# Expert stage of a decoder layer: split distance, whole f32 down weights, place of the row sums

## The chip, the cores and the metric

The program runs on one core of one Trainium2 chip. The metric is the device time of one execution in microseconds (us); less is better. Engines: PE (matmul; PEld loads its stationary side), DVE (vector), ACT (scalar), POOL (GpSimd), SP (issues most DMAs).

## The reference

A layer of [RMSNorm, four token mixers, gated merge, residual] and [RMSNorm, hierarchical mixture of experts, residual], then a last RMSNorm, on 512 tokens of width 1024, all in float32. The change touches the experts alone:

```python
gates = ...                      # (tokens, 16): top-1 group, top-2 experts in it
for e in range(N_EXPERTS):       # 16 experts, hidden 512
    h = jax.nn.silu(xt @ w_g[e]) * (xt @ w_u[e])
    out = out + gates[:, e:e + 1] * (h @ w_d[e]).astype(f32)
```

Each token goes to two experts only, so the kernel gathers the tokens of an expert and leaves the others out.

## The kernel before

The stages follow each other: mixers, merge, output projection, routing (to about 656 us), experts, closing part. Five engine programs are written out by hand; they meet through semaphores, and each works strictly in its written order.

**Split numbers.** The weights come in float32. A product is made of f16 halves: ACT writes the high half of a weight chunk (line 853, times 64), DVE the rest (line 1737, chunk minus high half), and `products` (lines 980 to 982) makes three f16 matmuls, high by high, high by low, low by high. The tokens x and the hidden values h are split the same way.

**Chunks.** The 16 experts' weights are 96 chunks of 128 x 2048 float32 (1 MB), listed in `STEPS`: for expert e two "g" (gate), two "u" (up), then two "d" (down) of expert e-1. Numbers: expert e's first g chunk is c = 6e-2 (for e above 0), its u chunks follow, then 6e+2 and 6e+3 are d of e-1. Before expert 14's u chunks the d chunks of 13 are taken first, so 84 and 85 are d of 13; 92, 93 are d of 14 and 94, 95 d of 15. A g or u chunk takes 16 x 3 matmuls of 96 columns (CAP = 96 places for tokens), a d chunk 4 x 3 of 512.

**Buffers and SP.** There are 12 stage slots (`NS`) for float32 chunks and six pairs of f16 halves (`NW`). `stage_load` (line 450) issues a chunk's DMA; before it SP waits until the slot's last chunk is split (`splits_ahead`), and loads are issued in order of c. From chunk 20 on the slot is that of c-12.

**ACT and DVE.** Both walk over the steps c. At step c they do the small work of that step, then `split(c + LOOK)`, with LOOK = 5. ACT's small work: after the second g chunk it waits for that chunk's products and makes the tanh (918); at the second u chunk it waits for the transposes of the next expert's x and writes its high halves (908); one step later the high half of h (928); after the second d chunk it waits for its products and copies y out (935; 939 for experts 14 and 15, whose rows stay on the chip). DVE's: x low halves (1844), h (1894, 1895), h low half (1849), y low halves (1859), the sums of rows (1854).

**PE.** At step c it waits for the split of c (and for x or h where a step begins with them), does the products and signals `chunk_used`. After the second u chunk it transposes the next expert's tokens (1322).

**Tokens.** POOL gathers an expert's tokens with an indirect DMA (580) and scatters its y rows of experts 0 to 13 to memory (588). At the end SP reads them back (494) in four groups of 128 tokens, and `add_rows(t)` adds two of them per token with their weights, at the last four steps c = 92 to 95, after that step's other work on DVE. Experts 14 and 15 come back by one-hot matmuls (`put_back`, 1367), which `add_last` (1916) adds; then the norm (897, 892, 1826, 1829) and the store (510).

Of the kernel before, what the change touches and what calls it, by code (L numbers as in the profile page):

```python
# [50 lines left out]
LOOK = 5  # L51
# [89 lines left out]

def steps_to(kind, e):

    return STEPS.index((kind, e, 1)) + 1
# [49 lines left out]
def build(nc, d, out):  # L196

    ctx = ExitStack()
    with ctx:
# [92 lines left out]
        def splits_ahead(c):  # L292

            return max((i + 1 for i in range(c) if SLOT[i] == SLOT[c]), default=0)
# [13 lines left out]
        hgT = [[view(19456 + 512 * i + 256 * j, KH * CAP // 2).bitcast(F16) for j in range(2)] for i in range(2)]  # L308
# [111 lines left out]
        def _(sp_):  # L420
# [47 lines left out]
            for c in range(READY, READY + FIRST):  # L468
                sp_.wait_ge(S("split_done"), splits_ahead(c))
# [10 lines left out]
            with sp_.If(fit):  # L480
                for c in range(READY + FIRST, len(STEPS)):
                    if splits_ahead(c):
                        sp_.wait_ge(S("split_done"), splits_ahead(c))
                    elif c == READY + FIRST:
                        sp_.wait_ge(S("x2_stored"), 16 * NT)
                    else:
                        sp_.wait_ge(S("token_full"), 2)
# [4 lines left out]
                for t in range(NT):  # L492
                    sp_.wait_ge(S("split_done"), len(STEPS) - NS + t + 1)
# [102 lines left out]
        def _(act):  # L596
# [252 lines left out]
            def split(c):  # L849
                act.wait_ge(S(f"stage_landed{SLOT[c]}"), landed(c))  # L850
                if c >= NW:
                    act.wait_ge(S("chunk_used"), c - NW + 1)
                act.activation(w_hi[c % NW], stage[c], ACT.Copy, scale=WSCALE).then_inc(S("hi_done"), 1)  # L853
# [48 lines left out]
            with act.If(fit):  # L902
# [10 lines left out]
                for c, (kind, e, hf) in enumerate(STEPS):  # L913
# [9 lines left out]
                    if STEPS[c - 1][0] == "u" and STEPS[c - 1][2]:  # L923
                        eh = STEPS[c - 1][1]
                        act.wait_ge(S("h_ready"), eh + 1)
                        if eh >= 2:
                            act.wait_ge(S("chunk_used"), steps_to("d", eh - 2))
                        act.activation(hgT[eh % 2][0], hid, ACT.Copy).then_inc(S("hhi_done"), 1)
                    if kind == "d" and hf:
# [3 lines left out]
                        for j in range(2):  # L933
                            if e < ROUTED:
                                act.activation(yout[e % 2][0:CAP, 512 * j:512 * (j + 1)], ps[4 + j][0:CAP, :], ACT.Copy,  # L935
                                               scale=1.0 / (WSCALE * HSCALE)).then_inc(S("y_out"), 1)
# [4 lines left out]
                    if FIRST <= c + LOOK < len(STEPS):  # L941
                        split(c + LOOK)
# [22 lines left out]
        def _(pe):  # L965
# [339 lines left out]
            with pe.If(fit):  # L1305
# [23 lines left out]
                for c, (kind, e, hf) in enumerate(STEPS):  # L1329
                    if kind == "d" and not hf:  # L1330
                        pe.wait_ge(S("hlo_done"), e + 1)
# [8 lines left out]
                    pe.wait_ge(S("split_done"), c + 1)  # L1340
                    if kind == "d":
                        v = [w[c % NW].rearrange("p (k n) -> p k n", k=2) for w in (w_hi, w_lo)]
                        hi, lo = (h.rearrange("p (k c) -> p k c", c=CAP) for h in hgT[e % 2])
# [627 lines left out]
```

## Time and profile before

| | us |
|---|---|
| median of 3 runs | 964.55 (960.51 to 964.68) |
| profiled execution, its own time | 964.39 |
| span of its trace | 962.6 |
| PE busy | 876.3 (91%) |
| DVE busy | 658.8 (68%) |
| ACT busy | 481.0 (50%) |
| mean granted clock of PE | 0.957 of 2.4 GHz |

Times in rows are microseconds from the span's start unless marked ns. A share of busy time is an average over stages with different limits. In a timeline "[0.98 <-DMA ...]" is idle time before the instruction and what ended it. DMA share is the mean over 16 DMA engines.

### The profile page before, as it was taken

What the parts mean: (1) busy time and instruction counts of PE and PEld (TensorE: products, weight loads), DVE (VectorE), ACT (ScalarE), POOL (GpSimd) and SP (SyncE); (2) the same over time, 40 slices, a digit from 0 to 9 for tenths busy, and PEclk for the clock granted to TensorE, in tenths of its full rate; (3) what the DMA queues carried; (4) which work ended last, traced back from release to release, by engine and by line L of the source; (5) the groups of instructions that cost most, each with busy time, mean ns of one, the idle gap of its engine ahead of it and who ended that gap; (6) DMA issues with size and microseconds to landing.
All of it is one profiled execution on the core that took longest, in us unless ns stands there. A gap on an engine that the chain in (4) does not pass through costs nothing.

```text
span 962.6 us, 19161 instructions
## 1 busy us (share of the span) xinstructions
PE 876.3 (91%) x8176; PEld 585.2 (61%) x8176; DVE 658.8 (68%) x877; ACT 481.0 (50%) x681; POOL 81.8 (8%) x89
## 2 busy tenths in 40 slices
PE   6999999999999998999999979948899999888683
PEld 4444794856756655444444439947687777776561
DVE  5668769632887766643453344466799999998878
ACT  5434473323554445233223223554597878787842
POOL 8000000003000000000000000000121232111100
PEclk9999999999999999999999999967899999999987
DMA  8711414526731012953432416374899999999852
GB/s 213 168 35 45 125 30 110 155 66 176 188 91 34 25 37 61 372 137 98 121 102 83 122 28 220 127 284 140 305 359 383 399 397 397 381 392 378 331 203 90
DMA packets 122607, 178.20 MB, mean 185 GB/s; under 512 B 13357, under 2 KB 98661, under 8 KB 114326
## 3 DMA queue, kind: packets, MB, share of 16 engines
q1 hardware_dynamic: 116272, 162.76, 49.6%
q0 software_dynamic: 5968, 13.61, 5.2%
q8 instruction: 66, 1.08, 0.5%
q10 hardware_dynamic: 278, 0.56, 0.2%
q14 instruction: 23, 0.19, 0.1%
HBM read 170.67 MB, written 14.39 MB: 192 GB/s over the span
## 4 chain that ended last, share of the span: by engine, by line
PE 64%; DVE 19%; DMA 7%; ACT 6%; issue 3%; DVEq 0%; SPq 0%; ACTq 0%; POOLq 0%
PE bank L980 17%; PE bank L982 17%; PE bank L981 17%; DVE arena L1737 10%; DMA arena<-in_moe_wu 6%; ACT arena L853 3%; PE bank L1193 3%; PE bank L1212 3%; PE bank L1087 1%; PE bank L1202 1%; DVE arena L1844 1%; DMA arena<-x_rows,token_of 1%; DVE arena L1854 1%; ACT arena L935 1%; PE bank L1284 1%
## 5 line engine op out<-in xcount | busy, mean ns | idle before, releaser
L980 PE MATMUL bank<-arena 128*128 128x96 f16 (+3 forms) x2336 | 510.0, 264 | 37.4 <-DVE arena L1844 26.4
L981 PE MATMUL bank<-arena 128*128 128x96 f16 (+3 forms) x2336 | 509.0, 264 | 0.0
L982 PE MATMUL bank<-arena 128*128 128x96 f16 (+3 forms) x2336 | 508.6, 264 | 0.3
L980 PEld LDWEIGHTS bank<-arena 128*128 128x128 f16 (+1 forms) x2336 | 238.2, 102 | 139.4 <-issue 34.1
L982 PEld LDWEIGHTS bank<-arena 128*128 128x128 f16 (+1 forms) x2336 | 237.4, 102 | 77.1 <-issue 1.7
L981 PEld LDWEIGHTS bank<-arena 128*128 128x128 f16 (+1 forms) x2336 | 237.5, 102 | 68.2 <-issue 1.6
L1737 DVE SCALAR_TENSOR_TENSOR arena<-arena 128x2048 f16<-128x2048 f32 x96 | 216.9, 2287 | 49.2 <-ACT arena L853 46.8
L853 ACT ACTIVATE arena<-arena 128x2048 f16<-128x2048 f32 x96 | 180.6, 1904 | 12.5 <-DMA arena<-in_moe_wu 5.5
L620 ACT ACTIVATE arena<-arena 128x1024 f16<-128x1024 f32 (+1 forms) x92 | 92.5, 1007 | 101.3 <-PE bank L982 73.2
L1482 DVE SCALAR_TENSOR_TENSOR arena<-arena 128x1024 f16<-128x1024 f32 (+1 forms) x91 | 103.5, 1163 | 11.7 <-ACT arena L620 10.1
L674 ACT ACTIVATE arena<-bank 128x512 f32<-128x512 f32 x35 | 20.8, 595 | 90.4 <-PE bank L982 90.3
L794 ACT ACTIVATE arena<-arena,nmx 128x128 f32<-128x128 f32 (+3 forms) x48 | 26.9, 561 | 61.4 <-DVE nmx L1682 61.4
L1728 DVE SCALAR_TENSOR_TENSOR arena<-arena,bank 128x512 f32<-128x512 f32 x24 | 16.4, 685 | 57.7 <-PE bank L982 57.6
L844 ACT ACTIVATE arena<-bank,half 128x512 f32<-128x512 f32 x24 | 16.3, 679 | 49.8 <-PE bank L982 49.8
L1679 DVE TENSOR_TENSOR arena<-bank,arena 128x128 f32<-128x128 f32 (+3 forms) x48 | 23.5, 489 | 22.5 <-PE bank L1193 18.8
L1193 PE MATMUL bank<-arena 64*128 64x128 f32 (+3 forms) x96 | 38.5, 482 | 0.0
L580 POOL DMA_INDIRECT arena<-x_rows,token_of x16 | 30.1, 1880 | 89.2 <-PE bank L1322 62.5
L1726 DVE SCALAR_TENSOR_TENSOR arena<-arena,bank 128x512 f32<-128x512 f32 x8 | 5.5, 686 | 46.4 <-PE bank L982 46.4
L1212 PE MATMUL bank<-arena 128*128 128x64 f32 x240 | 32.5, 267 | 1.2 <-ACT arena L803 1.1
L1212 PEld LDWEIGHTS bank<-arena 128*128 128x128 f32 x240 | 30.5, 191 | 3.0 <-ACT arena L803 2.2
L588 POOL DMA_INDIRECT y_rows<-arena,row_of x14 | 20.6, 1474 | 125.6 <-ACT arena L935 125.6
L1571 DVE MAX8 m<-arena 128x8 f32<-128x256 f32 (+2 forms) x48 | 26.7, 557 | 0.9
(275 smaller groups left out, 726.5 us busy)
## 6 DMA issues: line engine op xcount, KB each, us to landing
arena<-in_moe_wg SPq DMA_DIRECT2D x32, 1024.0 KB, 17.4
arena<-in_moe_wu SPq DMA_DIRECT2D x32, 1024.0 KB, 16.1
arena<-in_moe_wd SPq DMA_DIRECT2D x32, 1024.0 KB, 23.6
arena<-in_w_gate SPq DMA_DIRECT2D x32, 512.0 KB, 4.0
arena<-in_w_in SPq DMA_DIRECT2D x31, 512.0 KB, 4.2
arena<-in_w_branch SPq DMA_DIRECT2D x32, 192.0 KB, 3.5
y_rows<-in_c_tab SPq DMA_DIRECT2D x4, 1024.0 KB, 12.5
arena<-in_w_out SPq DMA_DIRECT2D x8, 512.0 KB, 5.3
```

Source lines behind the costliest of these rows:

```text
L580: pool.indirect_dma_start(out=xg[0:CAP, :], out_offset=None, in_=x2_rows, in_offset=bass.IndirectOffsetOnAxis(ap=token_of[0:CAP, e:e + 1], ...
L620: act.activation(*split_views(c, c_hi), ACT.Copy, scale=WSCALE).then_inc(S("c_hi_done"), 1)
L794: act.activation(pr[n % 3][:, 0:nk], lg[n % 3][:, 0:nk], ACT.Exp, bias=nmx[:, n % 4:n % 4 + 1], accum_out=lsum[:, (n // HEADS) % 2, n % HE ...
L853: act.activation(w_hi[c % NW], stage[c], ACT.Copy, scale=WSCALE).then_inc(S("hi_done"), 1)
L980: pe.matmul(outb, lhs[0], rhs[0], start=first, stop=False, skip_group_check=True)
L981: pe.matmul(outb, lhs[0], rhs[1], start=False, stop=False, skip_group_check=True)
L982: return pe.matmul(outb, lhs[1], rhs[0], start=False, stop=last_, skip_group_check=True)
L1193: pe.matmul(lgb[n % 2][:, 0:(i + 1) * P], q[r, h // 2, i * P:(i + 1) * P], k[r, h // 2, 0:(i + 1) * P], start=True, stop=True).then_inc(S( ...
L1212: last = pe.matmul(ps[6 + g % 2][:, h * HD:(h + 1) * HD], pT[:, n % 2, b * P:(b + 1) * P], v[:, b, h * HD:(h + 1) * HD], start=(b == 0), s ...
L1482: ins = stt(lo, src, WSCALE, hi, ALU.mult, ALU.subtract)
L1571: link(dve.max(out=m8[:, :], in_=sel[i]))
L1737: tell("split_done", stt(w_lo[c % NW], stage[c], WSCALE, w_hi[c % NW], ALU.mult, ALU.subtract))
```

## The change

- **Split distance.** `SPLITS_AT[c]` lists which chunks are split at step c. For c below 48 that is up to c+5. From 48 on it is up to c + max(2, 5 - (c - 48) // 8): 5 at 48 to 55, 4 at 56 to 63, 3 at 64 to 71, 2 from 72.
- **Whole down chunks.** The d chunks of odd experts (`WHOLE`, 16 of 96, the first 14 and 15, the last 94 and 95) are not split. PE waits for the landing itself and multiplies f32 by f32, four matmul calls of 512 columns, with h of odd experts kept in f32 (`hid_whole`). `CUT` numbers the remaining 80 chunks for semaphores and f16 buffers. The slot of a whole chunk is free when its products are done (`slot_free` gives the semaphore and its value). The high and low copies of h are made for even experts alone, in one buffer pair; the scale 1/64 falls away for odd experts.
- **Rows.** `add_rows` 0 and 1 come at step 92, 2 at 93, 3 at 94, none at 95.

```diff
@@ -48,7 +48,7 @@
 FIRST = 5
-LOOK = 5
+LOOK, LOOK_END = 5, 2
 WARM = 12
@@ -141,6 +141,17 @@
+WHOLE = [kind == "d" and e % 2 == 1 for kind, e, _ in STEPS]
+CUT = [c for c in range(len(STEPS)) if not WHOLE[c]]
+SPLITS_AT, _c = {}, FIRST
+for _at in range(len(STEPS)):
+    _upto = _at + (LOOK if _at < len(STEPS) // 2 else max(LOOK_END, LOOK - (_at - len(STEPS) // 2) // 8))
+    SPLITS_AT[_at] = [_i for _i in range(_c, min(_upto + 1, len(STEPS))) if not WHOLE[_i]]
+    _c = max(_c, _upto + 1)
 def steps_to(kind, e):
@@ -289,9 +300,12 @@
-        def splits_ahead(c):
-            return max((i + 1 for i in range(c) if SLOT[i] == SLOT[c]), default=0)
+        def slot_free(c):
+            last = max((i for i in range(c) if SLOT[i] == SLOT[c]), default=None)
+            if last is None:
+                return None
+            return ("chunk_used", last + 1) if WHOLE[last] else ("split_done", CUT.index(last) + 1)
@@ -305,7 +319,8 @@
         yout = [arena[:, 9216 + D * i:9216 + D * (i + 1)] for i in range(2)]
-        hgT = [[view(19456 + 512 * i + 256 * j, KH * CAP // 2).bitcast(F16) for j in range(2)] for i in range(2)]
+        hgT = [view(19456 + 192 * j, KH * CAP // 2).bitcast(F16) for j in range(2)]
+        hid_whole = view(19456 + 512, KH * CAP)
         yg = [view(STAGE[SLOT[len(STEPS) - NS + t]], 2, D) for t in range(NT)]
@@ -466,7 +481,7 @@
             for c in range(READY, READY + FIRST):
-                sp_.wait_ge(S("split_done"), splits_ahead(c))
+                sp_.wait_ge(S("split_done"), slot_free(c)[1])
                 stage_load(c)
@@ -479,8 +494,8 @@
                 for c in range(READY + FIRST, len(STEPS)):
-                    if splits_ahead(c):
-                        sp_.wait_ge(S("split_done"), splits_ahead(c))
+                    if slot_free(c):
+                        sp_.wait_ge(S(slot_free(c)[0]), slot_free(c)[1])
                     elif c == READY + FIRST:
@@ -490,7 +505,11 @@
                 for t in range(NT):
-                    sp_.wait_ge(S("split_done"), len(STEPS) - NS + t + 1)
+                    c = len(STEPS) - NS + t
+                    if WHOLE[c]:
+                        sp_.wait_ge(S("chunk_used"), c + 1)
+                    else:
+                        sp_.wait_ge(S("split_done"), CUT.index(c) + 1)
                     sp_.dma_start(yg[t], y_rows.rearrange("(j t p) n -> t p j n", j=2, p=P)[t]
@@ -847,10 +866,11 @@
             def split(c):
+                i = CUT.index(c)
                 act.wait_ge(S(f"stage_landed{SLOT[c]}"), landed(c))
-                if c >= NW:
-                    act.wait_ge(S("chunk_used"), c - NW + 1)
-                act.activation(w_hi[c % NW], stage[c], ACT.Copy, scale=WSCALE).then_inc(S("hi_done"), 1)
+                if i >= NW:
+                    act.wait_ge(S("chunk_used"), CUT[i - NW] + 1)
+                act.activation(w_hi[i % NW], stage[c], ACT.Copy, scale=WSCALE).then_inc(S("hi_done"), 1)
@@ -922,10 +942,11 @@
                         eh = STEPS[c - 1][1]
-                        act.wait_ge(S("h_ready"), eh + 1)
-                        if eh >= 2:
-                            act.wait_ge(S("chunk_used"), steps_to("d", eh - 2))
-                        act.activation(hgT[eh % 2][0], hid, ACT.Copy).then_inc(S("hhi_done"), 1)
+                        if eh % 2 == 0:
+                            act.wait_ge(S("h_ready"), eh + 1)
+                            if eh >= 2:
+                                act.wait_ge(S("chunk_used"), steps_to("d", eh - 2))
+                            act.activation(hgT[0], hid, ACT.Copy).then_inc(S("hhi_done"), 1)
                     if kind == "d" and hf:
@@ -933,13 +954,13 @@
                                 act.activation(yout[e % 2][0:CAP, 512 * j:512 * (j + 1)], ps[4 + j][0:CAP, :], ACT.Copy,
-                                               scale=1.0 / (WSCALE * HSCALE)).then_inc(S("y_out"), 1)
+                                               scale=1.0 / ((1.0 if e % 2 else WSCALE) * HSCALE)).then_inc(S("y_out"), 1)
                             else:
...
                                                scale=slotw[0:CAP, e - ROUTED:e - ROUTED + 1]).then_inc(S("y_out"), 1)
-                    if FIRST <= c + LOOK < len(STEPS):
-                        split(c + LOOK)
+                    for i in SPLITS_AT[c]:
+                        split(i)
                     if c == len(STEPS) // 2:
@@ -1328,7 +1349,10 @@
                     if kind == "d" and not hf:
-                        pe.wait_ge(S("hlo_done"), e + 1)
+                        if e % 2:
+                            pe.wait_ge(S("h_ready"), e + 1)
+                        else:
+                            pe.wait_ge(S("hlo_done"), e // 2 + 1)
                         if 1 <= e <= ROUTED:
@@ -1337,17 +1361,28 @@
                             pe.wait_ge(S("h_ready"), e - 1)
-                    pe.wait_ge(S("split_done"), c + 1)
+                    if WHOLE[c]:
+                        pe.wait_ge(S(f"stage_landed{SLOT[c]}"), landed(c))
+                        v = stage[c].rearrange("p (k n) -> p k n", k=2)
+                        h = hid_whole.rearrange("p (k c) -> p k c", c=CAP)
+                        for k in range(2):
+                            for j in range(2):
+                                last = pe.matmul(y_bank(e)[j][0:CAP, :], h[:, 2 * hf + k, :], v[:, k, 512 * j:512 * (j + 1)],
+                                                 start=hf == 0 and k == 0, stop=hf == 1 and k == 1, skip_group_check=True)
+                        last.then_inc(S("chunk_used"), 1)
+                        continue
+                    i = CUT.index(c)
+                    pe.wait_ge(S("split_done"), i + 1)
                     if kind == "d":
-                        v = [w[c % NW].rearrange("p (k n) -> p k n", k=2) for w in (w_hi, w_lo)]
-                        hi, lo = (h.rearrange("p (k c) -> p k c", c=CAP) for h in hgT[e % 2])
+                        v = [w[i % NW].rearrange("p (k n) -> p k n", k=2) for w in (w_hi, w_lo)]
+                        hi, lo = (h.rearrange("p (k c) -> p k c", c=CAP) for h in hgT)
                         for k in range(2):
...
                     else:
-                        v = [w[c % NW].rearrange("p (k n) -> p k n", k=4) for w in (w_hi, w_lo)]
+                        v = [w[i % NW].rearrange("p (k n) -> p k n", k=4) for w in (w_hi, w_lo)]
                         hi, lo = xgT
@@ -1733,8 +1768,9 @@
             def split(c):
-                dve.wait_ge(S("hi_done"), c + 1)
-                tell("split_done", stt(w_lo[c % NW], stage[c], WSCALE, w_hi[c % NW], ALU.mult, ALU.subtract))
+                i = CUT.index(c)
+                dve.wait_ge(S("hi_done"), i + 1)
+                tell("split_done", stt(w_lo[i % NW], stage[c], WSCALE, w_hi[i % NW], ALU.mult, ALU.subtract))
@@ -1845,8 +1881,8 @@
                 def h_lo(e):
-                    dve.wait_ge(S("hhi_done"), e + 1)
-                    tell("hlo_done", tt(hgT[e % 2][1], hid, hgT[e % 2][0], ALU.subtract))
+                    dve.wait_ge(S("hhi_done"), e // 2 + 1)
+                    tell("hlo_done", tt(hgT[1], hid, hgT[0], ALU.subtract))
@@ -1874,7 +1910,9 @@
                     link(tt(slotw[0:CAP, :], slotw[0:CAP, :], got[:, 4, ROUTED:], ALU.add))
-                    link(ts(slotw[0:CAP, :], slotw[0:CAP, :], 1.0 / (WSCALE * HSCALE * W16), None, ALU.mult))
+                    link(ts(slotw[0:CAP, :], slotw[0:CAP, :], 1.0 / (HSCALE * W16), None, ALU.mult))
+                    for e in range(ROUTED, NE, 2):
+                        link(ts(slotw[0:CAP, e - ROUTED:e - ROUTED + 1], slotw[0:CAP, e - ROUTED:e - ROUTED + 1], 1.0 / WSCALE, None, ALU.mult))
                     link(ts(slotv[0:CAP, 0, :], got[:, 1, :], -float(NOWHERE), float(NOWHERE), ALU.mult, ALU.add))
@@ -1892,22 +1930,27 @@
                         link(stt(sgr, sgr, 1.0, ps[b0][:, 0:KH * CAP], ALU.add, ALU.mult))
-                        tell("h_ready", stt(hid, sgr, 0.5 * HSCALE / WSCALE ** 2, ps[b0 + 1][:, 0:KH * CAP],
+                        if e >= 3 and e % 2:
+                            dve.wait_ge(S("chunk_used"), steps_to("d", e - 2))
+                        tell("h_ready", stt(hid_whole if e % 2 else hid, sgr, 0.5 * HSCALE / WSCALE ** 2, ps[b0 + 1][:, 0:KH * CAP],
                                             ALU.mult, ALU.mult))
-                    if STEPS[c - 1][0] == "u" and STEPS[c - 1][2]:
+                    if STEPS[c - 1][0] == "u" and STEPS[c - 1][2] and STEPS[c - 1][1] % 2 == 0:
                         h_lo(STEPS[c - 1][1])
...
                         y_lo(e)
-                    if FIRST <= c + LOOK < len(STEPS):
-                        split(c + LOOK)
+                    for i in SPLITS_AT[c]:
+                        split(i)
                     if c == 1:
...
                             tell("onehot_ready", ts(onehot_T[i][0:CAP, :], tok_iota[0:CAP, :], slotv[0:CAP, 1, ROUTED + i:ROUTED + i + 1], None, ALU.is_equal))
-                    if c >= len(STEPS) - NT:
-                        add_rows(c - len(STEPS) + NT)
+                    if c == len(STEPS) - NT:
+                        add_rows(0)
+                        add_rows(1)
+                    elif len(STEPS) - NT < c < len(STEPS) - 1:
+                        add_rows(c - len(STEPS) + NT + 1)
```

## Rows read from the trace of the kernel before

**Rows 1.** The stretches view: us, each engine's busy us (x), clock, DMA share, GB/s.

```profile
715.00:731.03 16.03, 15.89 (x260) 13.39 (x258) 15.72 (x12) 13.41 (x13) 3.49 (x3) 1.00 1.02 386
...
881.30:899.60 18.30, 13.96 (x179) 10.62 (x177) 16.06 (x11) 13.98 (x12) 3.19 (x3) 1.00 1.02 386
```

**Rows 2.** Timeline of DVE, one expert: start, duration, line, [idle before it].

```profile
812.46 8.90 DVE L1737 SCALAR_TENSOR_TENSOR arena<-arena 128x2048 f16<-128x2048 f32 x4 [0.28 <-ACT arena L853]
821.27 1.02 DVE L1844 TENSOR_TENSOR arena<-bank,arena 128x384 f16<-128x384 f32 x2
822.21 0.54 DVE L1894 SCALAR_TENSOR_TENSOR arena<-arena,bank 128x384 f32<-128x384 f32 x1
```

**Rows 3.** Timeline of ACT, experts 12 to 15.

```profile
850.01 1.91 ACT L853 ACTIVATE arena<-arena 128x2048 f16<-128x2048 f32 x1 [0.98 <-DMA arena<-in_moe_wg]
851.83 0.85 ACT L908 ACTIVATE arena<-bank 128x384 f16<-128x384 f32 x2
...
857.49 1.91 ACT L853 ACTIVATE arena<-arena 128x2048 f16<-128x2048 f32 x1 [0.70 <-DMA arena<-in_moe_wu]
859.31 1.06 ACT L935 ACTIVATE arena<-bank 96x512 f32<-96x512 f32 x2
...
864.19 0.47 ACT L918 ACTIVATE arena<-bank 128x384 f32<-128x384 f32 x1
...
905.45 1.91 ACT L853 ACTIVATE arena<-arena 128x2048 f16<-128x2048 f32 x1 [1.18 <-DMA arena<-in_moe_wg]
...
910.71 1.91 ACT L853 ACTIVATE arena<-arena 128x2048 f16<-128x2048 f32 x1 [0.54 <-DMA arena<-in_moe_wu]
```

**Rows 4.** The DMA view, issues at 665 to 670, then at 870 to 900.

```profile
arena<-in_moe_wg SPq DMA_DIRECT2D x1, 1024.0 KB, 4.7
...
arena<-in_moe_wg SPq DMA_DIRECT2D x2, 1024.0 KB, 26.3
```

**Rows 5.** Timeline of SP's queue, 700 to 710.

```profile
702.13 2.58 SPq L450 DMA_DIRECT2D arena<-in_moe_wd  x2
706.54 2.54 SPq L450 DMA_DIRECT2D arena<-in_moe_wg  x2
```

**Rows 6.** PE: chain of waits, then timelines, then the records of line 1087.

```profile
705.03 1.00 PE bank L1322 x8
...
863.84 0.44 PE L1322 MATMUL bank<-cst,arena 96*128 96x96 f32 x2
...
898.55 0.38 PE L980 MATMUL bank<-arena 128*96 128x512 f16 x1
898.76 0.38 PE L981 MATMUL bank<-arena 128*96 128x512 f16 x1
...
78.34 1.88 PE L1087 MATMUL bank<-arena 128*128 128x512 f32 x4
...
L1087 PE MATMUL bank<-arena x28: 592/592/592, 78.3 to 89.9; 128*128 128x512 f32 x28
```

**Rows 7.** The stretches view, two falls of the clock.

```profile
870.00:874.00 4.00, 1.01 (x20) 0.83 (x20) 3.97 (x5) 1.60 (x3) 0.00 (x0) 0.99 0.93 304
874.00:877.00 3.00, 3.00 (x41) 3.00 (x39) 2.20 (x2) 1.74 (x3) 0.00 (x0) 0.50 0.73 289
...
912.00:920.00 8.00, 4.07 (x52) 4.07 (x53) 7.80 (x9) 5.50 (x6) 0.00 (x0) 0.50 0.64 228
```

**Rows 8.** Timelines of the closing part: ACT, PE, DVE.

```profile
923.42 1.28 ACT L920 ACT_TABLE_LOAD   x1
...
939.07 1.26 ACT L939 ACTIVATE arena<-bank,slotw 96x512 f16<-96x512 f32 x2 [4.92 <-PE bank L982]
...
915.93 0.26 PE L980 MATMUL bank<-arena 128*128 128x96 f16 x1 [7.61 <-DVE arena L1844]
...
942.74 1.41 DVE L1859 SCALAR_TENSOR_TENSOR arena<-bank,slotw,arena 96x512 f16<-96x512 f32 x2
...
946.69 2.87 DVE L1916 TENSOR_TENSOR arena<-bank,arena 128x512 f32<-128x512 f32 x4
```

## The prediction

> **What bounds the kernel now.** I read the busy time by stretches first, then the timelines of DVE, ACT and SP in order of time, because in the expert stage all engines and the DMA are busy and shares name no bound. The stage is 96 chunks of 1 MB (c = 0 to 95), consumed in order. I name P(c) the end of chunk c's products on PE. At 715 DVE is busy 15.72 of 16.03 us, and the rows repeat every 16.03 us: DVE sets that pace [rows 1]. Its six splits are 2.2 to 2.29 us each, and the rest is the two x halves (1.01), 0.54 twice for h and about as much for its low half [rows 2]. At 881.3 the same work takes 18.3 us and DVE has slack [rows 1]. The reader should now look at ACT: its splits there end waits for a DMA, and the one of the second chunk of expert 12 (850.01) and that of expert 15 (905.45, three experts on) are 55.4 us apart, 18.5 us each [rows 3]. So from about 845 the landings set the pace. They fell behind gradually: a chunk issued at 665 us lands after 4.7 us, one issued at 870 to 900 after 26.3 us, while SP issues as soon as a slot is free [rows 4]. A queue that grows steadily is served at full rate all along; the second half would be paced by landings whatever DVE does, and a faster DVE only empties the lead sooner. After 910.71, when chunk 91 lands, there remain split, products and the closing part.
>
> **Units of the sum.** Chunk 73 lands at 857.49 (ACT's wait ends [rows 3]) and its products end at 863.84, where the transposes of the next x begin [rows 6]: landing to products' end is 6.35 us, of it 1.91 on ACT, 2.29 on DVE, the rest, 2.15, the products of a "g" or "u" chunk with their start (I take 2.04 where PE runs on). A "d" chunk has 12 matmuls at 0.216 (898.55 to 898.76 [rows 6]), 2.6 us, so about 0.55 more: 6.9.
>
> **Down weights of odd experts in f32.** This removes 16 ACT splits (30.5 us), 16 DVE splits (16 x 2.29 = 36.6) and 8 pairs of copies of h (8 x 0.5 on each). It adds PE time: the trace has f32 matmuls of 512 columns, four records in 1.88 us with the last one's tail, and as the 14 calls of line 1087 (seven for each of two gates) leave 28 records, a call is two records of 0.43 us [rows 6]. Four calls are 3.43 us a chunk against 2.6, +0.84, 13.4 us over 16 chunks. The stationary side here is 96 wide, not 128; bounds: as three f16 products (2.6 us a chunk) and twice the row (6.9); I take the row. PE's own work per expert is 4 x 2.04 + 1.0 transposes + 5.2 = 14.4 us, 16.1 with f32, 15.25 on average: less than 16.03 and much less than 18.5. So in the first half the stage becomes PE-bound at 15.25 and the gain is 0.8 us an expert, some 6 us by 845; but landings take over there, so it is worth nothing at the end. What it costs is on SP. A whole chunk's slot is free after its products, not after its split, five chunks earlier. Chunk 26 reuses the slot of chunk 14. It is issued at 702.13 [rows 5]; now it waits for P(14) = 706.03 (transposes' end, 705.03 + 1.00 [rows 6]) + 3.43 = 709.5, and on SP chunk 27 (P(15), 712.9) and 28, 29 (706.54 before [rows 5]) stand behind it. At that time little is in flight, so the DMA queue runs dry for some microseconds which it never gets back, being saturated from there on. Chunks 26 to 28 land 5 to 6 us later; some of the gap is filled by x and y rows that would have cost time anyway. Bounds 0 and 6.5 us; I take +4 on every later landing. Later such waits of SP meet a queue up to 26 us deep [rows 4] and cost nothing. So P(73) = 863.9 + 4 = 867.9. Were DMA no limit at all, PE alone would need 59 chunks x 15.25 / 6 = 150 us from P(14): P(73) = 859.5. That is the lower bound.
>
> **Distance 5 to 2.** Today, once landings set the pace, ACT and DVE block on chunk c+5 before they do the small steps that PE needs at c+1; at 915.93 PE had waited 7.61 us so [rows 8]. With 2 they block less early. But the split of c+2 on ACT stands behind ACT's own wait for P(c) in three places of each expert: tanh after the second g chunk, the x halves after the second u, and the y copies after the second d. Behind these, ACT's split, DVE's split and the products of c+2 run one after the other, while PE has only chunk c+1 (2.04 to 2.6 us). From P(73) on, with the pieces 0.47 (tanh), 1.06 (two y copies), 0.43 (second x half) [rows 3] and 1.0 (transposes), the chain is:
> - to P(75), whole: 1.0 + 6.9 = 7.9. To P(77): 1.05 + 6.35 = 7.4. To P(79): 0.47 + 6.35 = 6.8
> - to P(81), split: 1.0 + 0.43 + 6.9 = 8.3. To P(83): 7.4. To P(85), whole, straight on PE: 6.9
> - to P(87): 7.4. To P(89): 1.43 + 6.35 = 7.8. To P(91): 0.47 + 1.5 (table load and square root, 923.42 [rows 8]) + 6.35 = 8.3
> - to P(93): h on DVE 1.1, split 2.3, products 2.6 = 6.0. To P(95), whole: 6.9
>
> Sum 81.1 us, where before P(73) to P(95) is 863.9 to 939.07 (ACT's wait for PE [rows 8]) = 75.2, and where one expert now takes about 22 us against 18.5 of the landings. The bound moves from the landings to this chain, and the last landing (four chunks after 910.71 at 3.1 us each, plus 4, so near 927) no longer matters. P(95) = 867.9 + 81.1 = 949.0, ten later.
>
> **Expert rows in the gaps.** Before, DVE adds the last rows after the low halves of y: 942.74 those halves start, 946.69 the final sums start, 7.6 us after P(95) [rows 8]. Now rows 2 and 3 are done while PE works on chunks 94 and 95 (6.9 us against 5.2). After P(95): first y copy 0.6, two low halves 1.4 [rows 8], four put-back matmuls 1.2 (estimate from 4 x 0.216 and a start): 3.2. That gives back 4.4 us, and the 15.9 us from 946.69 to 962.6 stay. The extra small DVE scaling of slotw at step 4 is 0.2 us beside PE's work; hidden.
>
> **The clock.** PE's granted clock fell to 1.2 GHz after it was busy 1.01 of 4 us (870 to 874) and after the wait at 908 to 916; it stayed there in 874 to 877 and 912 to 920 [rows 7]. The wait at 908, part of the 75.2, goes away with its slow products, which the chain already leaves out. The new chain leaves PE idle about 3 us after P(75), P(81), P(85) and 4 us after P(89). I count one fall, 1.7 us, bounds 0 and 8.
> The Trainium skill, page "TensorE: Matmul & The Clock Gate", section "HAM oscillation — how this bites in real kernels", speaks against the change: a loop that waits in each round can pay the slow clock each round. By it all four waits would be followed by products at half speed and the time would be about 6 us longer than my sum. The rows show both: a fall at 874, and full clock from 881.3 to 899.6 though PE was idle for 4.3 us of it in all [rows 1, 7].
>
> **Sum.** +10.0 - 4.4 + 1.7 = +7.3: span 962.6 to 969.9, and with the 1.8 us around it (964.39 profiled) 971.7 us. The profiled run agrees with the median of 964.55 within 0.2 us. I say 971.5.
>
> **Rivals.**
> - A, faster: the landings still set the pace, that is, ACT and DVE get a chunk done in the 18.5 us rhythm despite the distance. For it: that is the stage's bound now. Against: the three hops per expert are plain sums of durations in the trace. Then P(91) = 910.7 + 4 + 6.35 = 921.1, P(93) 927.1, P(95) 934.0, +3.2 + 15.9 = 953.1, time 954.9. It decides where the landings' period exceeds 22 us, which no row shows. 0.13.
> - B, no difference: the chain holds, but SP's wait costs no landing, or DMA recovers it: P(73) between 859.5 and 863.9, no clock fall, time 961.5 to 966; 965 stands for it. For it: depth of the queue later. Against: the short flights near 700 us. 0.22.
> - C, much slower: the f32 calls cost nearer twice the row in the whole chunks (+3.4 for each of the six in the last chain, part hidden) or the clock falls after every wait: 979. 0.08.
> - The forecast, 0.57.
>
> That the change does not do what it says is not among them: the orders of splits and waits follow from the diff.
> The likeliest is 971.5, its own range 967 to 977. The range to hold 8 in 10 is 961 to 978, down to rival B's lower bound and up to an almost full clock loss. Over 0.5% (4.8 us; less than that a measurement of this kernel can't tell from nothing): faster 0.13 (A), within 0.22 (B), slower 0.65 (forecast and C).
>
> **What would show it.** Right: in the last 100 us ACT's splits wait for PE and for no DMA; the period of the transposes from 866 on is about 22 us; chunk 26's load is issued near 709.5; f32 products take 3.4 us a chunk; the final sums start 3 us after the last products. Wrong: ACT still waits for in_moe_wu there, or the transposes are 18 to 19 us apart; or the f32 chunks take 2.6 or 6.9 us.

## The result, and the profile after

| | before | changed |
|---|---|---|
| median, us | 963.97 (960.51 to 964.68, 4 runs) | 980.64 (976.09 to 983.97, 4 runs) |
| ratio | | 1.0177, 95% interval 1.0121 to 1.0233 |
| second measurement, ratio | | 1.0195, interval 1.0170 to 1.0220 |
| profiled execution, its time / span | 964.39 / 962.6 | 977.88 / 976.1 |
| busy PE / DVE / ACT | 876.3 / 658.8 / 481.0 | 889.9 / 620.7 / 451.6 |

The change is slower by 17 us where 7 were forecast. PE gained 13.6 us of work, DVE lost 38.1, ACT 29.4 (the part on the f32 weights gives 13.4, 40.6 and 34.5). That the loss is not PE's added work is shown by the kernel with the whole chunks alone (first group of experiments).

ACT's timeline of the changed kernel (line 873 is the split, 938 the tanh, 928 the x halves, 956 the y copies), to be held against [rows 3]:

```profile
862.00 1.91 ACT L873 ACTIVATE arena<-arena 128x2048 f16<-128x2048 f32 x1 [2.11 <-DMA arena<-in_moe_wu]
...
876.41 1.08 ACT L956 ACTIVATE arena<-bank 96x512 f32<-96x512 f32 x2 [2.39 <-PE bank L1370]
877.38 3.70 ACT L873 ACTIVATE arena<-arena 128x2048 f16<-128x2048 f32 x2
883.92 0.49 ACT L938 ACTIVATE arena<-bank 128x384 f32<-128x384 f32 x1 [2.83 <-PE bank L1003]
884.30 3.70 ACT L873 ACTIVATE arena<-arena 128x2048 f16<-128x2048 f32 x2
891.36 0.97 ACT L928 ACTIVATE arena<-bank 128x384 f16<-128x384 f32 x2 [3.35 <-PE bank L1343]
892.22 3.70 ACT L873 ACTIVATE arena<-arena 128x2048 f16<-128x2048 f32 x2
900.92 1.08 ACT L956 ACTIVATE arena<-bank 96x512 f32<-96x512 f32 x2 [5.00 <-PE bank L1003]
...
915.34 1.08 ACT L956 ACTIVATE arena<-bank 96x512 f32<-96x512 f32 x2 [4.62 <-PE bank L1370]
```

Chunk 73 is the last that ACT waits for: it lands at 862.00 (857.49 before). From then on no split waits for a DMA. ACT's waits of 868 to 956, added up (us, times, longest), are for PE but for one of 1.7 us for DVE; those of the three places are:

```profile
ACT arena L928 <- PE bank L1343: 12.7, 3, 4.8
ACT arena L938 <- PE bank L1003: 9.9, 3, 4.6
...
ACT arena L956 <- PE bank L1370: 7.0, 2, 4.6
...
ACT arena L956 <- PE bank L1003: 5.0, 1, 5.0
```

In each of the three places the split of c+2 follows the small work at once: tanh at 883.92, split at 884.30. The chain of waits, pieces on DVE and PE (1343 are the transposes, 1370 the f32 products):

```profile
868.51 1.00 PE bank L1343 x8
869.50 6.88 PE bank L1370 x16
...
879.32 2.30 DVE arena L1773
...
890.80 1.01 PE bank L1343 x8
...
896.51 0.42 PE bank L1001
...
908.39 6.92 PE bank L1370 x16
...
923.91 1.20 PE bank L1343 x8
```

From transposes to transposes it is 890.80 - 868.51 = 22.3 us (forecast: about 22), against 18.5 of the landings. Two whole chunks take 6.88 us (forecast 2 x 3.43). PE is busy for 16.69 of these 22.29 us and DVE for 13.89: no engine is the bound, the order of their work is.

```profile
868.51:890.80 22.29, 16.69 (x218) 11.71 (x217) 13.89 (x10) 12.05 (x11) 1.91 (x2) 1.00 0.96 371
```

On SP the pair of whole chunks 26, 27 is issued 14.8 us after the pair before it, where it was 7.2 us (694.95 to 702.13; the latter in [rows 5]), and four more chunks stand behind it:

```profile
693.82 2.53 SPq L465 DMA_DIRECT2D arena<-in_moe_wu  x2
708.63 3.81 SPq L465 DMA_DIRECT2D arena<-in_moe_wd  x2
712.49 0.95 SPq L465 DMA_DIRECT2D arena<-in_moe_wg  x2
713.49 1.07 SPq L465 DMA_DIRECT2D arena<-in_moe_wu  x2
```

The DMA queue runs dry meanwhile. In 704 to 708 the DMA share (second number from the right) is 0.94 in the kernel before (first row) and 0.02 in the changed one (second row):

```profile
704.00:708.00 4.00, 4.00 (x43) 3.10 (x40) 4.00 (x3) 3.97 (x4) 1.17 (x1) 1.00 0.94 269
...
704.00:708.00 4.00, 4.00 (x19) 2.15 (x17) 4.00 (x5) 2.98 (x4) 1.85 (x1) 1.00 0.02 3
```

The landings take over earlier than the forecast's 845. From 720 to 795 an expert takes 15.0 us (transposes at 720.14 and, five experts on, 795.22; forecast 15.25), PE is busy throughout, and then ACT waits 5.69 us for a landing; the next two experts take 20.2 and 19.1 us.

```profile
797.52 1.91 ACT L873 ACTIVATE arena<-arena 128x2048 f16<-128x2048 f32 x1 [5.69 <-DMA arena<-in_moe_wg]
```

The stretches view (clock is the third number from the right) shows the falls of the clock in the chain. They follow gaps of PE that end at 896.5 (2.1 us long), 920.6 (3.2) and 938.4 (3.7); no fall follows the gaps that end at 881.7 (3.0), 888.6 (2.5) and 906.2 (3.2):

```profile
896.00:900.00 4.00, 3.49 (x11) 1.82 (x12) 2.65 (x2) 0.00 (x0) 0.00 (x0) 0.69 1.02 332
920.00:924.00 4.00, 3.40 (x50) 3.41 (x51) 2.74 (x2) 0.01 (x1) 0.00 (x0) 0.68 0.29 117
936.00:940.00 4.00, 1.61 (x22) 1.62 (x23) 3.96 (x2) 3.61 (x3) 0.00 (x0) 0.81 0.04 15
```

The closing part, as in [rows 8]: the y copies of expert 15 follow PE (5.61 us wait), then DVE. Rows 0 and 1 start at 945.57, rows 2 and 3 at 952.18, and the low halves of y only at 957.45:

```profile
955.41 1.26 ACT L960 ACTIVATE arena<-bank,slotw 96x512 f16<-96x512 f32 x2 [5.61 <-PE bank L1370]
...
945.57 5.24 DVE L1890 SCALAR_TENSOR_TENSOR arena<-arena,wsel 128x1024 f32<-128x1024 f32 x4
950.85 1.40 DVE L1895 SCALAR_TENSOR_TENSOR arena<-bank,slotw,arena 96x512 f16<-96x512 f32 x2
952.18 5.24 DVE L1890 SCALAR_TENSOR_TENSOR arena<-arena,wsel 128x1024 f32<-128x1024 f32 x4
957.45 1.40 DVE L1895 SCALAR_TENSOR_TENSOR arena<-bank,slotw,arena 96x512 f16<-96x512 f32 x2
959.98 2.87 DVE L1959 TENSOR_TENSOR arena<-bank,arena 128x512 f32<-128x512 f32 x4 [1.13 <-PE bank L1402]
```

### The profile page after: what moved, and what is told of

It reads as the page before. It is cut to its first block, busy times and chain, and to the rows that moved or that the text cites. A ratio compares the mean times of both kernels' runs of the same rounds, so it can differ in the third digit from the quotient of the medians.

```text
span 976.1 us, 18970 instructions
## 1 busy us (share of the span) xinstructions
PE 889.9 (91%) x8112; PEld 582.7 (60%) x8112; DVE 620.7 (64%) x854; ACT 451.6 (46%) x657; POOL 80.1 (8%) x89
## 4 chain that ended last, share of the span: by engine, by line
PE 70%; DVE 12%; DMA 10%; ACT 5%; issue 2%; SPq 1%; DVEq 0%; ACTq 0%; POOLq 0%
PE bank L1001 18%; PE bank L1002 17%; PE bank L1003 17%; DMA arena<-in_moe_wu 6%; DVE arena L1773 5%; PE bank L1214 3%; PE bank L1370 3%; DMA arena<-in_moe_wg 3%; PE bank L1233 3%; ACT arena L873 3%; PE bank L1108 1%; PE bank L1223 1%; DVE arena L1890 1%; DMA arena<-x_rows,token_of 1%; SPq L465 1%
## 5 line engine op out<-in xcount | busy, mean ns | idle before, releaser
L1001 PE MATMUL bank<-arena 128*128 128x96 f16 (+3 forms) x2272 | 486.5, 261 | 39.6 <-DVE arena L1773 23.1
L1002 PE MATMUL bank<-arena 128*128 128x96 f16 (+3 forms) x2272 | 485.8, 261 | 0.0
L1003 PE MATMUL bank<-arena 128*128 128x96 f16 (+3 forms) x2272 | 485.5, 261 | 0.0
L1001 PEld LDWEIGHTS bank<-arena 128*128 128x128 f16 (+1 forms) x2272 | 230.1, 101 | 137.1 <-issue 36.6
L1003 PEld LDWEIGHTS bank<-arena 128*128 128x128 f16 (+1 forms) x2272 | 229.6, 101 | 71.3 <-issue 1.9
L1002 PEld LDWEIGHTS bank<-arena 128*128 128x128 f16 (+1 forms) x2272 | 229.6, 101 | 65.2 <-issue 4.2
L1773 DVE SCALAR_TENSOR_TENSOR arena<-arena 128x2048 f16<-128x2048 f32 x80 | 181.2, 2288 | 91.9 <-ACT arena L873 91.9
L873 ACT ACTIVATE arena<-arena 128x2048 f16<-128x2048 f32 x80 | 150.4, 1904 | 21.1 <-DMA arena<-in_moe_wg 13.9
L1517 DVE SCALAR_TENSOR_TENSOR arena<-arena 128x1024 f16<-128x1024 f32 (+1 forms) x91 | 103.5, 1163 | 11.7 <-ACT arena L639 10.1
L1370 PE MATMUL bank<-arena 128*96 128x512 f32 x128 | 56.3, 593 | 0.0
L1370 PEld LDWEIGHTS bank<-arena 128*96 128x96 f32 x128 | 20.5, 165 | 30.0 <-issue 29.8
L599 POOL DMA_INDIRECT arena<-x_rows,token_of x16 | 27.0, 1685 | 124.4 <-PE bank L1343 97.4
```

The source lines that it names most:

```text
L599: pool.indirect_dma_start(out=xg[0:CAP, :], out_offset=None, in_=x2_rows, in_offset=bass.IndirectOffsetOnAxis(ap=token_of[0:CAP, e:e + 1], ...
L873: act.activation(w_hi[i % NW], stage[c], ACT.Copy, scale=WSCALE).then_inc(S("hi_done"), 1)
L1001: pe.matmul(outb, lhs[0], rhs[0], start=first, stop=False, skip_group_check=True)
L1002: pe.matmul(outb, lhs[0], rhs[1], start=False, stop=False, skip_group_check=True)
L1003: return pe.matmul(outb, lhs[1], rhs[0], start=False, stop=last_, skip_group_check=True)
L1370: last = pe.matmul(y_bank(e)[j][0:CAP, :], h[:, 2 * hf + k, :], v[:, k, 512 * j:512 * (j + 1)], start=hf == 0 and k == 0, stop=hf == 1 and ...
```

## The experiments

Ratios are to the kernel before, run on the same chip beside each; 0.001 is 0.96 us. The first four kernels ran on one chip, the next four on a second, the last three on a third. "Changed" is the changed kernel.

| kernel | ratio | 95% interval |
|---|---|---|
| distance alone | 1.0159 | 1.0132 to 1.0187 |
| whole chunks alone | 1.0016 | 1.0002 to 1.0030 |
| rows alone | 1.0011 | 0.9996 to 1.0026 |
| changed, ends at distance 3 | 1.0013 | 0.9998 to 1.0028 |
| changed, PE's gaps filled | 1.0134 | 1.0106 to 1.0162 |
| changed, ACT splits first | 0.9960 | 0.9942 to 0.9978 |
| ends at 3, first pair split | 0.9960 | 0.9941 to 0.9978 |
| both repairs (splits first, first pair split) | 0.9907 | 0.9887 to 0.9927 |
| changed, ACT splits first, no whole chunk | 0.9955 | 0.9940 to 0.9969 |
| both repairs, rows back | 0.9907 | 0.9883 to 0.9932 |
| both repairs, only expert 15 whole | 0.9883 | 0.9861 to 0.9905 |

My theory: a chain of ACT's wait, ACT's split, DVE's split and products at distance 2, with clock falls in its gaps. Rival 1: the f32 products, 13.4 us more on PE. Rival 2: SP's late issue and the landings.

**1. Each part alone.** Distance alone:

```diff
-LOOK = 5
+LOOK, LOOK_END = 5, 2      # SPLITS_AT as in the change, but of all chunks
```

> The kernel before with the shrinking split distance alone (to 2 from step 72); all chunks split, rows as before. Theory (a chain of ACT's wait for the products, ACT split, DVE split, products, three times an expert, and clock falls in its gaps): 11 to 16 us slower than before, experts 13 to 15 at 21 to 23 us each, and ACT's splits there wait for PE and not for a DMA. Rival 1 (the f32 down weights cost the time on PE): within 2 us of before. Rival 2 (SP's late issue of chunk 26 and the landings carry it): within 2 us of before.

15.3 us slower. From transposes to transposes it is 22.9 us (865.72 to 888.64). ACT's waits from 868 to 945 (942, 925 and 915 are its y copies, tanh and x halves) are for PE again, but for one of 3.2 us for DVE:

```profile
ACT arena L942 <- PE bank L989: 11.1, 3, 4.7
ACT arena L925 <- PE bank L989: 8.8, 3, 3.6
ACT arena L915 <- PE bank L1329: 8.7, 2, 5.3
```

Whole chunks alone (the change with `LOOK, LOOK_END = 5, 5` and the rows at their old place):

> The kernel before with the 16 whole f32 down chunks alone; distance 5 throughout, rows as before. Theory: the landings shift by 4 us at chunk 26 and stay shifted, the last two chunks need no split, so 1 to 5 us slower than before. Rival 1 (f32 products, 0.85 us longer per chunk, 16 times, on PE's path): about 13 us slower. Rival 2 (landings): 4 to 5 us slower and the rest of the loss in no part alone.

1.5 us slower (0.2 to 2.9). Rival 1 falls: PE's 13.4 us do not appear. The late issue is there (the pair 26, 27 is again 14.8 us behind the pair before it); but from the transposes after chunk 73 to the last products it then takes about 74 us (872.2 to 946.1) where it took 75.2.

Rows alone:

```diff
-                    if c >= len(STEPS) - NT:
-                        add_rows(c - len(STEPS) + NT)
+                    if c == len(STEPS) - NT:
+                        add_rows(0)
+                        add_rows(1)
+                    elif len(STEPS) - NT < c < len(STEPS) - 1:
+                        add_rows(c - len(STEPS) + NT + 1)
```

> The kernel before with the moved row sums alone (0 and 1 at step 92, 2 at 93, 3 at 94). Theory: DVE is busy with rows until the low halves of the last y either way; these end 2.6 us later than before, and the put-back matmuls follow them: between 0 and 2 us slower. Rival (the move gives back what was forecast, 4 us): 3 to 4 us faster.

1.1 us slower (-0.4 to 2.5): beside distance 5 the move gives nothing. The three parts sum to 1.86%, the whole change to 1.77 or 1.95%.

**2. Distance 3.**

```diff
-LOOK, LOOK_END = 5, 2
+LOOK, LOOK_END = 5, 3
```

> The changed kernel with the distance shrinking to 3 and no further. Theory (at 3 the split of c+3 has two chunks of products beside it, so the chain of about 22 us an expert becomes shorter than the landings' 18.5): 0 to 4 us faster than the kernel before, ACT's splits wait for DMA again after 870. Rival 1 (f32 products): still over 10 us slower than before. Rival 2 (landings): 4 us slower.

One step of distance is worth 16 to 18 us. ACT waits for landings again, and its waits for PE in the three places are fewer (868 to 945):

```profile
ACT arena L873 <- DMA arena<-in_moe_wu: 6.8, 4, 2.1
...
ACT arena L938 <- PE bank L1003: 5.7, 2, 4.7
```

The gain over the kernel before did not come: 1.3 us slower (-0.2 to 2.7) where 0 to 4 faster was expected. SP's issues show why: the two rows are again 14.8 us apart, chunks 24 and 25, then 26 and 27.

```profile
700.17 2.53 SPq L465 DMA_DIRECT2D arena<-in_moe_wu  x2
714.98 3.81 SPq L465 DMA_DIRECT2D arena<-in_moe_wd  x2
```

**3. The first whole pair.** The same kernel, but chunks 14 and 15 are split:

```diff
-WHOLE = [kind == "d" and e % 2 == 1 for kind, e, _ in STEPS]
+def whole(e):
+    return e % 2 == 1 and e > 1
...
+WHOLE = [kind == "d" and whole(e) for kind, e, _ in STEPS]
...      # h of expert 1 gets a pair of f16 buffers where hid_whole lies until expert 3
```

> The variant that ends at distance 3, but with the first pair of whole chunks (14 and 15, down weights of expert 1) split as before; 14 whole chunks are left. Theory (SP's wait for the products of chunk 14 holds up chunk 26 and lets the DMA queue run dry for 4 to 6 us which the landings never get back): chunk 26 is issued 6 us earlier, landings 4 us earlier, time 3 to 6 us faster than the end-at-3 variant and 3 to 7 us faster than before. Rival (the queue recovers, the later landings are due to the pace of DMA): no difference to the end-at-3 variant.

0.53% or 5.1 us faster than with 16 whole chunks (the intervals do not touch), 3.9 us faster than before. The pair is issued 7.5 us after the one before it:

```profile
694.04 3.00 SPq L474 DMA_DIRECT2D arena<-in_moe_wu  x2
701.49 2.58 SPq L474 DMA_DIRECT2D arena<-in_moe_wd  x2
```

From the stage's first transposes (near 654) to those after chunk 73 it takes 215.5 us in the profile with sixteen whole chunks and 209.4 with fourteen (209.8 before). Rival 2 is thus right for one term, of about 5 us, and wrong for the rest.

**4. The order on ACT.** The changed kernel, distance 2 kept:

```diff
                 for c, (kind, e, hf) in enumerate(STEPS):
+                    for i in SPLITS_AT[c]:
+                        split(i)
                     if kind == "g" and hf:
                         act.wait_ge(S("chunk_used"), steps_to("g", e))
...
-                    for i in SPLITS_AT[c]:
-                        split(i)
                     if c == len(STEPS) // 2:
```

> The changed kernel, distances kept at 2, but at each step ACT does its split of c+2 before, not after, its small work and that work's wait for the products of c. Theory (ACT's order, split behind the wait, makes the chain): 11 to 17 us faster than the changed kernel, 3 us faster to 3 us slower than before. Rival (a distance of 2 is too short whatever the order on ACT, since DVE and PE follow one another): still 8 us or more slower than before.

From 1.0177 or 1.0195 to 0.9960: 21 to 23 us, more than the 11 to 17 expected, and 3.9 us faster than before. Not one instruction is added or taken away. Three to four of these microseconds lie ahead of the chain: from the stage's first transposes to those after chunk 73 it is 211.6 us, against 214.7 and 216.0 in the two profiles of the changed kernel; the order is changed at the distances 5 to 3 too. And the clock is 0.98 on average from 866 to 936, so what its falls cost is in this gain as well. ACT's timeline: the split of chunk 79 (877.06, waits for its landing) now precedes the tanh (878.88), and the splits wait for DMAs again.

```profile
877.06 1.91 ACT L873 ACTIVATE arena<-arena 128x2048 f16<-128x2048 f32 x1 [0.32 <-DMA arena<-in_moe_wu]
878.88 0.47 ACT L940 ACTIVATE arena<-bank 128x384 f32<-128x384 f32 x1
881.02 1.91 ACT L873 ACTIVATE arena<-arena 128x2048 f16<-128x2048 f32 x1 [1.67 <-DMA arena<-in_moe_wd]
884.44 1.91 ACT L873 ACTIVATE arena<-arena 128x2048 f16<-128x2048 f32 x1 [1.51 <-DMA arena<-in_moe_wd]
```

**5. The clock.** The changed kernel with matmuls of constants in PE's gaps, into columns 384 to 511 of the bank that PE is filling, which nobody reads:

```diff
+FILL = {77: 40, 79: 32, 83: 40, 87: 40, 89: 8, 91: 48}
...
+                    for _ in range(FILL.get(c, 0)):
+                        pe.matmul(ps[2 * (e % 2) + (kind == "u")][:, 4 * CAP:512], earlier, allones,
+                                  start=False, stop=False, skip_group_check=True)
                     pe.wait_ge(S("split_done"), i + 1)
```

> The changed kernel with idle f16 products put before PE's waits at steps 77, 79, 83, 87 and 91 (32 to 48 of 128 columns, 1.8 to 2.7 us at full clock; 8 at step 89), written to columns that nothing reads. Theory (three clock falls in the gaps cost 4 to 5 us in the last chain): granted clock 1.00 from 870 to 960 and 3 to 5 us faster than the changed kernel, ratio to before near 1.013. Rival (the clock is not on the path, the chain alone carries all): no gain, or 1 to 2 us slower since PE finishes its filling late.

1.0134: 4 to 6 us faster than the changed kernel. Its interval overlaps the wide one of the first measurement and lies below that of the second (1.0170 to 1.0220). In its profile the clock is full from 866 to 950 (two of the stretches of 14 us), and the chain from transposes to last products takes 82.4 us where it was 86.9. This profiled execution, 971.5, is the fastest of its six (up to 978.74):

```profile
894.00:908.00 14.00, 12.64 (x157) 9.21 (x158) 5.78 (x4) 5.17 (x5) 0.95 (x1) 1.00 1.00 376
...
922.00:936.00 14.00, 11.57 (x236) 10.86 (x234) 10.01 (x7) 10.08 (x9) 0.00 (x0) 1.00 0.75 296
```

The changed kernel measured again, beside the last three kernels of the table, with a second profile:

> The changed kernel once more, on the chip of these three. Both theories: ratio to before 1.015 to 1.020; with it the chain from the transposes near 868 to the last products is 85 to 89 us, of which each fall of the clock after 890 explains 1 to 2.

1.0195, and 88.1 us from transposes to last products, as expected. Its profiled execution took 982.38. The clock falls four times in its chain, at 885.9, 909.8, 924.4 and 943.9, each time behind one of the gaps of 3.0 to 3.7 us, and from 886 to 942 it is 0.80 to 0.89 on average (first and last stretch):

```profile
886.00:900.00 14.00, 10.27 (x137) 8.73 (x134) 9.41 (x8) 8.66 (x7) 0.96 (x1) 0.89 1.01 413
...
928.00:942.00 14.00, 9.62 (x158) 8.89 (x155) 8.42 (x8) 10.23 (x10) 0.00 (x0) 0.80 0.78 301
```

**6. What whole chunks and rows are worth in the repaired kernel.** Both repairs together:

> Both repairs on the changed kernel at distance 2: first pair split, ACT's split ahead of its small work. Theory: the two add, 5 to 9 us faster than before. Rival: as the split-first variant alone, within 3 us of before.

0.9907, 9.0 us faster than before: they add (3.9 for the order relative to before, 5.1 for the pair). Without whole chunks at all (splits first, distance 2, rows moved):

> All chunks split (no f32 products), distance shrinking to 2, ACT's split ahead of its small work, rows moved. Theory: landings as before, but chunks 94 and 95 need a split each and PE's last steps are behind it: 4 to 6 us slower than the variant with both repairs, so 1 to 5 us faster than before. Rival (f32 down weights bring nothing once the landings set the pace): equal to the variant with both repairs, 9 us faster than before.

4.6 us slower than that. The trace shows why, and it is no landing: ACT's splits of chunks 92 to 95 (at 912.84 and 918.67) wait for no DMA, and the high half of chunk 95 is ready at 920.6. But DVE's part of that split stands behind the moved rows 0 and 1 and the y halves of expert 14 (1861 are the rows, 1866 the y halves, 1744 the split), and PE waits 5.94 us for it, from 925.91 to 931.85:

```profile
922.92 5.24 DVE L1861 SCALAR_TENSOR_TENSOR arena<-arena,wsel 128x1024 f32<-128x1024 f32 x4
928.19 1.41 DVE L1866 SCALAR_TENSOR_TENSOR arena<-bank,slotw,arena 96x512 f16<-96x512 f32 x2
929.52 2.28 DVE L1744 SCALAR_TENSOR_TENSOR arena<-arena 128x2048 f16<-128x2048 f32 x1
```

With the rows back at steps 92 to 95:

> The variant with both repairs (first pair split, ACT's split first, distance 2), with the row sums back at steps 92 to 95. Theory: the last rows stand behind the low halves of y again, in place of the wait for the put-back matmuls: within 2 us of that variant (0.9907 of before). Rival (the forecast's 4 us): 3 to 4 us slower than it.

No difference, within the 3 us that the two intervals leave, so the rival's 3 to 4 us are hardly possible. With expert 15's down weights alone whole:

```diff
-    return e % 2 == 1 and e > 1
+    return e == 15
...      # odd experts below 15 use the second pair of f16 buffers
```

> The variant with both repairs, but only expert 15's down weights whole; all other chunks split. Theory: what whole chunks bring is the last pair, which needs no split after landing; the other 12 only empty DVE's queue earlier in a stage that landings bound: within 2 us of the variant with both repairs. Rival (the others count through DVE time): 4 us or more slower than it.

0.9883, 11.3 us faster than before and the fastest of all. The step from fourteen whole chunks to these two is 2.3 us faster, but the intervals overlap (0.9861 to 0.9905, 0.9887 to 0.9927), so it is shown only that the other twelve bring no gain. The direct comparison for the last pair is with the kernel without any whole chunk, on the same chip: 0.9955 against 0.9883, 6.9 us, and the intervals do not touch. By the trace above, what f32 brings there is that DVE's split of chunk 95 no longer stands behind the rows and the y halves. No run isolates this: whether all chunks split, with the rows after that split, would be as fast was not tested.

## Why the prediction was right or wrong

The direction, the mechanism and the place were right; the size was not, and the time lies above the range. Term by term, in the profiled execution (976.1 - 962.6 = 13.5 us, where 7.3 were forecast):

- **Entry, right in size, within a wide spread.** SP's wait: chunk 26 issued at 708.63 (forecast 709.5), and the queue ran dry as forecast. P(73), the start of the transposes: 868.51 against 867.9, +4.7 for +4.0. The comparison of step 3 prices it at 5.1. A single profile says less than that: from the stage's first transposes to these it is 214.7, 216.0 and 212.4 us in the three profiles of the changed kernel (the filled one differs only after 876), against 209.8 before, so +2.6 to +6.2.
- **Chain, right but for the clock.** From 868.51 to 955.41 it is 86.9 us; the hops gave 81.1. The profile with filled gaps has 82.4 us from its transposes (P(73) at 866.3) to the last products (948.7), so the hops are right to 1.3 us. Of the 5.8 us that are too many, 4.9 lie in three of the eleven hops, those with the slow clock: to P(81) 10.1 us for 8.3 (890.80 to 900.92), to P(87) 8.6 for 7.4 (915.34 to 923.91), to P(91) 10.2 for 8.3 (932.06 to 942.31).
- **The clock term, the failed step.** "I count one fall, 1.7 us, bounds 0 and 8." Three fell in the chain (at 897.5, 921.4 and 938.5) and four in the second profile, and the filling is worth 4 to 6 us. I took full clock in 881.3 to 899.6 as a sign that such gaps are harmless; but one row of one expert was thin evidence. I also left out the gaps before P(79) and P(81), of 2.5 and 2.1 us, and behind the second of them the clock fell. The Trainium skill's rule (page "TensorE: Matmul & The Clock Gate", section "HAM oscillation — how this bites in real kernels"), that a loop which waits in each round can pay each time, put the cost at 6 us over my sum, 7.7 in all. The second profile agrees with the rule, with a fall behind each of the four waits that I named and a chain 7.0 us above the hops; in the first it is only two of these four, and 5.8 us. Both are nearer to the rule than to my one fall.
- **Rows, the second miss.** The prediction set rows 2 and 3 (5.2 us) against chunks 94 and 95 (6.9 us). DVE is only free 3.4 us after P(91) (945.57), and rows, y halves of expert 14 and rows again need 11.9 us from there, while P(95) comes 9.8 us after. So the low halves start 2.0 us after P(95) instead of 0.6, and the final sums 4.6 instead of 3.2. With the 0.2 us by which the rest is longer, 2.8 us are given back, not 4.4. Beside distance 5, or with ACT's splits first, the move is worth nothing that could be measured.
- **Spread.** Entry 4.7, chain 11.7 and tail -2.8 make these 13.5 us. The forecast had 4.0, 5.9 + 1.7 and -4.4: clock and hops make 4.1 us of the miss, rows 1.6, entry 0.6. The other 3 us up to the 16.7 between the medians are between executions: the median of the changed kernel lies 2.8 us above its profiled execution. The second profile's span is 4.5 us longer than the first's, of which 2.9 are there before the chain begins (transposes at 871.46 for 868.51) and 1.2 in it, so the falls of the clock in the chain are not the main part of that spread; what makes the rest was not tested.
- **Rival C, at 979,** had the nearest time, for one of its two causes: the clock falls behind each of the four long waits in the second profile; the other, f32 calls near twice the row, did not happen (6.88 us for two chunks). It was given 0.08.
- **Rival A** needed landings that stay the bound. With the order on ACT changed they nearly do: the period of the transposes is 17.6 us (865.80 to 883.40), and the time is 960.15 where A had 954.9.
- **The value of f32 before the landings take over** was nothing at the end, as said, though they took over at 797 and not near 845. What was not said is that the last pair pays: 6.9 us in the kernel with ACT's splits first, by the traces because a split on DVE goes away that stands behind the moved rows.

The chances were 0.57 for the forecast and 0.08 for C. Two of the four executions of the changed kernel (976.09 and 977.88) lie inside the range; the median of the second measurement, 983.25, is further out than that of the first.

## What to carry to other kernels

A software pipeline's distance is safe only together with the order inside a step: before shortening it, write down for each engine what its work for c+d stands behind, and add up that chain; if it is longer than the period, either keep the distance or put the look-ahead work ahead of the waits, which added no instruction here and turned a loss of 17 us into a gain of 4. The same holds for any other work that is moved: the row sums, put ahead of DVE's last split, cost PE 5.9 us in the kernel without whole chunks. When a buffer is released by a later event than before, look for the one place where the queue behind it is empty: one pair of 1 MB loads issued 7 us late cost 5 us to the end; for the twelve whole chunks after it no loss that size is seen (0.9907 with them, 0.9883 without).

## What the runs showed of the hardware

- In the changed kernel PE has six gaps of 2.1 to 3.7 us from 868 to 940. The clock fell behind three of them in one profile and four in another (0.68 to 0.89 on average in stretches of 4 to 14 us), and not behind others of the same length (3.2 us at 906, full clock after it). With 208 matmuls of 128 columns in these gaps it stayed at 1.00 in the profile, and the kernel was 4 to 6 us faster.
- An issue of two 1 MB loads that came 7.6 us later let the DMA share fall to 0.02 in 704 to 708 (0.94 before), and the landings did not make it up: about 5 us to the end.
- Matmuls of f32 with a 96-wide stationary side cost as much as with 128: 0.43 us per record of 512 columns (16 in 6.88 us; before, 28 in 12.18 us), two records a call.
